# A last down product with tokens on the partitions

## What is computed

```python
def swiglu_2(h, w_in, w_out):
    gate, up = jnp.split(h @ w_in, 2, axis=-1)
    return (jax.nn.silu(gate) * up) @ w_out

x = x + 0.5 * swiglu_2(rmsnorm(x, ffn2_norm[l]), ffn2_w_in[l], ffn2_w_out[l])
return rmsnorm(x, final_norm)        # x * rsqrt(mean(x*x over 1024) + 1e-6) * final_norm
```

## Time and profile before

| | us |
|---|---|
| median of 3 runs (lowest, highest) | 1096.36 (1095.93, 1096.79) |
| the profiled execution's own time | 1097.15 |
| its span, first to last instruction | 1095.4 |
| PE busy, of the span | 1079.4 (99%) |
| DVE busy | 780.0 (71%) |
| ACT busy | 619.1 (57%) |
| POOL busy | 201.7 (18%) |
| mean granted TensorE clock, core 0 | 0.994 |

### The profile page before, as it was taken

The page is one execution under the profiler, slowest core; times in us unless marked ns, Lnnn a source line. Parts: engine busy times, 40 slices in busy tenths (PEclk is TensorE's granted clock), DMA queues, the critical chain, the costliest instruction groups (busy, mean ns, idle before and its releaser), DMA issues.

```text
span 1095.4 us, 17872 instructions
## 1 busy us (share of the span) xinstructions
PE 1079.4 (99%) x6282; PEld 945.1 (86%) x6282; DVE 780.0 (71%) x1097; ACT 619.1 (57%) x947; POOL 201.7 (18%) x213
## 2 busy tenths in 40 slices
PE   8999999998999999999999999999999999999997
PEld 6888888887888888888888888889988898888886
DVE  6866667687797666768666676788867669666664
ACT  7655544564676555447555545755655557555541
POOL 4311100026031111011111100133201012111100
PEclk9999999998999999999999999999999999999998
DMA  8755566552246555556555654655455546655561
GB/s 281 276 193 186 180 192 192 176 168 99 98 158 212 189 190 191 176 174 215 190 190 189 189 187 163 212 186 194 158 190 177 189 155 193 210 188 188 180 194 39
DMA packets 55571, 200.02 MB, mean 183 GB/s; under 512 B 6304, under 2 KB 6304, under 8 KB 55392
## 3 DMA queue, kind: packets, MB, share of 16 engines
q1 hardware_dynamic: 54576, 196.11, 54.8%
q0 software_dynamic: 512, 2.65, 0.6%
q10 hardware_dynamic: 432, 0.57, 0.2%
HBM read 198.26 MB, written 1.05 MB: 182 GB/s over the span
## 4 chain that ended last, share of the span: by engine, by line
PE 93%; DVE 3%; POOL 1%; ACT 1%; DMA 1%; issue 0%; ACTq 0%; DVEq 0%; POOLq 0%
PE pair L1247 53%; PE pair L1248 27%; PE pair L1241 4%; PE pair L1243 4%; PE pair L1242 4%; DVE x_hl L817 1%; DVE w_lo L811 1%; PE pair L1460 1%; DMA x<-x_in 1%; POOL x_sq L395 1%; POOL x_sq L387 1%; PE pair L1470 0%; DVE x L828 0%; PE pair L1523 0%; PE pair L1565 0%
## 5 line engine op out<-in xcount | busy, mean ns | idle before, releaser
L811 DVE TENSOR_TENSOR w_lo<-w_raw,w_hi 128x1024 fp32r<-128x1024 f32 x369 | 462.2, 1259 | 230.4 <-ACT w_hi L463 229.8
L1247 PE MATMUL pair<-x_hl,w_hi 128*128 128x512 f32 x1728 | 604.2, 395 | 2.6 <-DVE x_hl L817 1.6
L463 ACT ACTIVATE w_hi<-w_raw 128x1024 fp32r<-128x1024 f32 x369 | 385.9, 1056 | 241.9 <-PE pair L1248 201.6
L1248 PE MATMUL pair<-x_hl,w_lo 128*128 128x256 f32 x1728 | 482.1, 279 | 0.0
L1247 PEld LDWEIGHTS pair<-x_hl,w_hi 128*128 128x128 f32 x1728 | 323.8, 187 | 79.2 <-DVE w_lo L811 2.0
L1248 PEld LDWEIGHTS pair<-x_hl,w_lo 128*128 128x128 f32 x1728 | 325.7, 188 | 0.1
L1247 PE MATMUL pair<-wide,w_hi 128*128 128x512 f32 x832 | 289.8, 393 | 0.0
L1248 PE MATMUL pair<-wide,w_lo 128*128 128x256 f32 x832 | 232.0, 279 | 0.0
L1247 PEld LDWEIGHTS pair<-wide,w_hi 128*128 128x128 f32 x832 | 155.9, 187 | 35.7
L1248 PEld LDWEIGHTS pair<-wide,w_lo 128*128 128x128 f32 x832 | 156.8, 188 | 0.0
L347 POOL TENSOR_TENSOR wide<-hid_b,wide 128x256 fp32r<-128x256 f32 x88 | 86.5, 984 | 374.7 <-ACT wide L525 374.7
(11 more groups left out here) (183 smaller groups left out, 846.4 us busy)
## 6 DMA issues: line engine op xcount, KB each, us to landing
w_raw<-stream SPq DMA_DIRECT2D x369, 512.0 KB, 4.2
const<-const_in POOLq DMA_DIRECT2D x1, 1248.0 KB, 8.6
w_raw<-stream SPq DMA_DIRECT2D x4, 256.0 KB, 5.6
out<-x_sq SPq DMA_DIRECT2D x4, 256.0 KB, 2.6
rows<-rows_in POOLq DMA_DIRECT2D x1, 576.0 KB, 10.6
x<-x_in ACTq DMA_DIRECT2D x2, 256.0 KB, 5.7
x<-x_in SPq DMA_DIRECT2D x2, 256.0 KB, 6.9
sgu_w<-sgu_w_in POOLq DMA_DIRECT2D x1, 512.0 KB, 13.6
```

The lines of the kernel that those rows point to most:

```text
L463: nc.scalar.activation(w_hi[:, slot, :], w_raw[:, slot, :], ACT.Copy).then_inc(w_hi_done, 1)
L811: nc.vector.tensor_tensor(w_lo[:, slot, :], w_raw[:, slot, :], w_hi[:, slot, :].bitcast(F32), ALU.subtract).then_inc(w_split, 1)
L1247: nc.tensor.matmul(dst, a_hi, b_hl.rearrange("p a s -> p (a s)"), start=first, stop=False, skip_group_check=True)
L1248: return nc.tensor.matmul(dst[:, 0:S], a_lo, b_hl[:, 0, :], start=False, stop=last, skip_group_check=True)
```

## The change

The down product of the last layer (p = 5) turns round; those of the other three layers stay.

- **Start.** TensorE transposes `x` (16 transposes of 128 x 128, into banks 0 to 3) and `rstd` (2, into bank 5). ACT copies the transposed `x` to `y_tok`, four times 128 x 512. DVE makes `r_col` = 0.5 x the first column of each transposed `rstd`.
- **Product.** Activations of 128 tokens are stationary, 512 weight columns move. For each half h of the features: 22 hidden chunks x 2 token groups x `three`. The host lays out the last 22 blocks to suit. Half 0 goes to banks 4 and 6, half 1 to banks 0 and 2. In half 1 the last four hidden chunks are done for the first token group, then for the second.
- **Half 0** is finished in the middle of the product: DVE adds `bank * r_col` to `y_tok`, ACT squares with an accumulated sum, DVE multiplies by the gain.
- **The end.** Per token group DVE makes the residual of half 1, ACT squares it with its sum, DVE multiplies by the gain; a root and its inverse are made for a column of 128 x 1; ACT scales half 0 and stores it from its own queue, DVE scales half 1 and SP stores it.
- The gain row comes by one more DMA of 512 KB from POOL, after `add_squares(5)`. The output has token rows. The sum over partitions, the diagonal and its product are gone.

```diff
@@ sync @@
-            for c in range(4):
-                sp.wait_ge(out_ready, c + 1)
-                sp.dma_start(out[:, 2 * c:2 * c + 2, :], x_sq[:, 2 * c:2 * c + 2, :]).then_inc(stored, 16)
+            for t in range(TT):
+                sp.wait_ge(out_ready, t + 1)
+                sp.dma_start(out[:, t, 512:D], out_tok[:, t, :]).then_inc(stored, 16)
@@ gpsimd @@
             add_squares(5)
+            pool.wait_ge(ya_split, KC)
+            pool.dma_start(gain_row, gain_in).then_inc(gain_loaded, 16)
             hidden_lo(3)
@@ scalar, ffn @@
+                def token_square(t, h):
+                    act.wait_ge(y_tok_made, TT * h + t + 1)
+                    nc.scalar.activation(q_tok[:, t, :], y_tok[:, t, 512 * h:512 * h + 512], ACT.Square,
+                                         accum_out=(end_part, end_sum)[h][:, t:t + 1]).then_inc(end_sq, 1)
+                def store(t):
+                    act.wait_ge(end_r_done, t + 1)
+                    act.wait_ge(end_gained, t + 1)
+                    nc.scalar.activation(y_tok[:, t, 0:512], y_tok[:, t, 0:512], ACT.Identity,
+                                         scale=end_r[:, t:t + 1]).then_inc(out_act_ready, 1)
+                    act.wait_ge(out_act_ready, t + 1)
+                    act.dma_start(out[:, t, 0:512], y_tok[:, t, 0:512]).then_inc(stored, 16)
                 if p == 5:
+                    for t in range(TT):
+                        act.wait_ge(x_T, t + 1)
+                        for h in range(2):
+                            nc.scalar.activation(y_tok[:, t, 512 * h:512 * h + 512], bank[2 * t + h][:, :],
+                                                 ACT.Copy).then_inc(x_T_copied, 1)
+                    for b in range(1, FC):
+                        split(n0 + UP_B + b + 3)
+                        if b == FC // 2:
+                            for t in range(TT):
+                                token_square(t, 0)
+                    for t in range(TT):
+                        token_square(t, 1)
+                        end_root_of(t)
+                        store(t)
+                    return
@@ vector, ffn @@
+                def token_residual(t, h):
+                    if h == 0:
+                        dve.wait_ge(w_used, n0 + UP_B + FC // 2)
+                    elif t == 0:
+                        dve.wait_ge(first_tokens, 1)
+                    else:
+                        dve.wait_ge(w_used, n0 + FFN_B)
+                    half = y_tok[:, t, 512 * h:512 * h + 512]
+                    nc.vector.scalar_tensor_tensor(half, bank[4 - 4 * h + 2 * t][:, :], r_col[:, t:t + 1], half, ALU.mult,
+                                                   ALU.add).then_inc(y_tok_made, 1)
+                    token_residual(0, 1)
+                    second_half_gain(0)
+                    end_scale(0)
+                    token_residual(1, 1)
+                    second_half_gain(1)
+                    store(0)
+                    end_scale(1)
+                    store(1)
@@ tensor @@
+            def tokens_down(n0):
+
+                pe.wait_ge(parts_added, 4 * FC - 2)
+                for t in range(TT):
+                    for c in range(KC):
+                        last = nc.tensor.transpose(bank[2 * t + c // 4][:, c % 4 * P:(c % 4 + 1) * P],
+                                                   x[:, c, t * P:(t + 1) * P], ident)
+                    last.then_inc(x_T, 1)
+                pe.wait_ge(parts_added, 4 * FC - 1)
+                for t in range(TT):
+                    last = nc.tensor.transpose(bank[5][:, t * P:(t + 1) * P], rstd[:, t * P:(t + 1) * P], ident)
+                last.then_inc(rT_done, 1)
+
+                def chunk(k, h, t):
+                    n, w = n0 + UP_B + (FC * h + k) // 2, slice(k % 2 * 512, k % 2 * 512 + 512)
+                    pe.wait_ge(w_split, n + 1)
+                    if h == 0 and t == 0:
+                        pe.wait_ge(hid_split, 3 * FC + k + 1)
+                    tok = slice(t * P, (t + 1) * P)
+                    return three(bank[4 - 4 * h + 2 * t][:, :], hid_hi[:, k, tok], hid_lo[:, k, tok], w_hi[:, n % RING, w],
+                                 w_lo[:, n % RING, w], k == 0, k == FC - 1)
+
+                for k in range(FC):
+                    for t in range(TT):
+                        if k == 0 and t == 1:
+                            pe.wait_ge(parts_added, 4 * FC)
+                        last = chunk(k, 0, t)
+                    if k % 2:
+                        last.then_inc(w_used, 1)
+                pe.wait_ge(x_T_copied, 2 * TT)
+                for k in range(FC - 4):
+                    for t in range(TT):
+                        last = chunk(k, 1, t)
+                    if k % 2:
+                        last.then_inc(w_used, 1)
+                for t in range(TT):
+                    for k in range(FC - 4, FC):
+                        last = chunk(k, 1, t)
+                        if t and k % 2:
+                            last.then_inc(w_used, 1)
+                    if t == 0:
+                        last.then_inc(first_tokens, 1)
...
-            for k in range(KC):
-                pe.wait_ge(x_sq_done, KC * 6 + k + 1)
-                for t in range(TT):
-                    last = nc.tensor.matmul(bank[4][:, t:t + 1], x_sq[:, k, t * P:(t + 1) * P], ones[:, 0:1],
-                                            start=(k == 0 and t == 0), stop=(k == KC - 1), skip_group_check=True)
-            last.then_inc(sumsq_done, 1)
```

More of the change, by code:

```diff
@@ L74, with build @@
 UNSEL, NEG, MASKED = -3.0e38, -2.0e38, -1.0e30
-def build(nc, stream, x_in, cols_in, rows_in, const_in, sgu_w_in, pool_w_in, out):
+def build(nc, stream, x_in, cols_in, rows_in, const_in, sgu_w_in, pool_w_in, gain_in, out):
     ctx = ExitStack()
@@ new lines, in end_scale @@
+                def end_scale(t):
+                    one = slice(t, t + 1)
+                    dve.wait_ge(end_sq, TT + t + 1)
+                    nc.vector.scalar_tensor_tensor(end_ms[:, one], end_sum[:, one], 1.0 / D, end_part[:, one], ALU.mult,
+                                                   ALU.add).then_inc(end_ms_done, 1)
+                    dve.wait_ge(end_root_done, t + 1)
+                    inv_root(end_ms[:, one], end_root[:, one], end_nt[:, one], end_r[:, one]).then_inc(end_r_done, 1)
@@ new lines, in store @@
+                def store(t):
+                    dve.wait_ge(end_r_done, t + 1)
+                    nc.vector.tensor_scalar(out_tok[:, t, :], out_tok[:, t, :], end_r[:, t:t + 1], None,
+                                            ALU.mult).then_inc(out_ready, 1)
+                if p == 5:
+                    dve.wait_ge(rT_done, 3)
+                    for t in range(TT):
+                        nc.vector.tensor_scalar(r_col[:, t:t + 1], bank[5][:, t * P:t * P + 1], 0.5, None,
+                                                ALU.mult).then_inc(half_r_made, 1)
+                    for b in range(1, FC):
+                        split(n0 + UP_B + b + 3)
+                        if b == FC // 2:
+                            dve.wait_ge(half_r_made, TT)
+                            dve.wait_ge(x_T_copied, 2 * TT)
+                            dve.wait_ge(gain_loaded, 16)
+                            for t in range(TT):
+                                token_residual(t, 0)
+                        if b == FC // 2 + 1:
+                            for t in range(TT):
+                                first_half_gain(t)
+                    dve.wait_ge(end_part_done, TT)
+                    token_residual(0, 1)
[6 more added lines that the diff above has]
+                    store(1)
+                    return
@@ L1219, in _ @@
             ffn(3, START[5], 5)
[L1221 to L1224, removed]
-            for t in range(TT):
[L1226 to L1233, removed]
-                                        ALU.mult).then_inc(out_ready, 1)
         @block.tensor
@@ L1353, in ffn @@
                         chunk(LEAD + j, j, i)
+                if p == 5:
+                    tokens_down(n0)
+                    return
                 for m in range(KC):
@@ L1560, in _ @@
             ffn(3, START[5], 5)
-            for k in range(KC):
-                pe.wait_ge(x_sq_done, KC * 6 + k + 1)
-                for t in range(TT):
-                    last = nc.tensor.matmul(bank[4][:, t:t + 1], x_sq[:, k, t * P:(t + 1) * P], ones[:, 0:1],
-                                            start=(k == 0 and t == 0), stop=(k == KC - 1), skip_group_check=True)
-            last.then_inc(sumsq_done, 1)
-            for t in range(TT):
-                pe.wait_ge(diagonal_done, t + 1)
-                last = nc.tensor.matmul(bank[5][:, t * P:(t + 1) * P], ones[:], newton[:, t * P:(t + 1) * P],
-                                        start=True, stop=True, skip_group_check=True)
-            last.then_inc(spread_done, 1)
 MIX1_SPLITS = (1, 2, 4, 7, 9)
@@ L1689 @@
     y = r.results[0]["out"]
```

(1 more changed line is left out.)

76 lines of the change are left out of this document (47 added, 29 removed).

## The result

The changed kernel took 1102.11 us (median of 22 runs, 1095.34 to 1105.59), the kernel before beside it 1096.14 (22 runs, 1095.66 to 1100.27). The ratio is 1.0041, 95% interval 1.003 to 1.0052. (A ratio with an interval is here an estimate from all runs of both kernels, not the quotient of the medians, which is 1.0054.) So the change costs 6 us between the medians and some 4.5 by the ratio, where a gain of 3.7, to 1092.7, was forecast. New as well is the scatter: 10 us between runs of the same program.

The account below looks back on a forecast made before the run. TensorE's stream was taken to bound the kernel up to the last down product's end, then a 12.1 us tail. Tail -4.56, product -1.08 and transposes +1.98 made -3.66, from 1096.36 to 1092.7 us; range 1091.5 to 1095.2.

Parts of the forecast that it names:

- Start: Start of the last down product: eighteen new transposes on TensorE at 0.11 us each add 1.98 us, with no wait.
- Product: Last down product: 264 matmuls at 0.227 us take 59.94 us against 61.02, a gain of 1.08.
- Cover: Beside the product: weight splits resume at about 1030.1, margin 2.8 us; mid-product they run 2.6 late of 6.0 allowed.
- Rival (a): Start or middle of the product: the weight ring runs dry behind ACT's waits, costing up to 2.4 us (1095.1); chance 0.06.
- Tail: After the last matmul: 7.34 us from when DVE may read it to the span's end; tail balance -4.56.
- Rival (b): Transposes at the product's start: TensorE's clock falls to half rate, losing 3.45 us (1096.15); chance 0.08.
- Rival (c): Early last layer: the gain's DMA delays the weight stream, TensorE stands for 4.8 us (1097.5); chance 0.04.
- Rival (d): Last down product: the turned form is no faster, giving 1093.8; counted within the forecast's 0.82.
- The first step of the prediction: Up to the last down product's end, 1083.30, only TensorE's stream counts: 176 pairs of 0.3467 us from 1022.28.
- the start of the sum: Start of the last down product at 1022.28 us, taken unchanged from the kernel before.

Follow-up runs that it names:

- e4: The kernel before, with the gain row's 512 KB DMA added, loaded and not used; median 1096.05 us against 1096.15, ratio 0.9988.
- e12: e2 with `ones` 64 bytes higher, again on a multiple of 64, and `wide` 128 bytes further from the weights; median 1095.9 us, ratio 0.9985 to before.
- e2: The changed kernel with every tile padded back to its old place; median 1093.0 us, ratio 0.9959 to before.
- e14: e12 with `wide` moved another 128 bytes on; median 1092.8 us, ratio 0.996 to before.
- e17: e2 with everything from `w_hi` on (split weights, `x_hl`, `wide`) 128 bytes higher, distances kept; median 1092.6 us, ratio 0.9965 to before.
- e9: The same kernel as e2, run again on another chip; median 1095.9 us, ratio 0.9984 to before.
- e1: The changed kernel unaltered, run again; median 1097.4 us (1093.1 to 1104.8), ratio 1.0001 to before.
- e11: e2 with only `ones` 32 bytes off, and `wide` 128 bytes further from the weights; median 1099.7 us, ratio 1.0023 to before.
- e10: The same kernel as e6, run again on another chip; median 1099.6 us, ratio 1.0017 to before.
- e15: e11 with `wide` moved another 128 bytes on; median 1096.3 us, ratio 0.9985 to before.
- e16: e2 with `x_hl` and all behind it 128 bytes on, and `wide` another 128 on; median 1102.1 us, ratio 1.0045 to before.
- e6: The changed kernel with only `ones` put back to its old place (padding also pushed `wide` by 128 bytes); median 1098.8 us, ratio 0.999 to before.
- e7: The kernel before with the six other moved tiles 32 bytes off, `ones` kept aligned, `wide` pushed 256 bytes; median 1096.7 us, ratio 0.997.
- e3: The kernel before with all seven moved tiles 32 bytes off (padding also pushed `wide` by 128 bytes); median 1105.3 us, ratio 1.0072.
- e5: The kernel before with only `ones` 32 bytes off (padding also pushed `wide` by 128 bytes); median 1104.7 us, ratio 1.0044.
- e8: e2 with one more, unused matmul of `ones` ahead of the second mixer's pairs; median 1096.5 us, ratio 0.9965 to before.
- e18: e12 with `wide` moved another 192 bytes on; median 1096.0 us, ratio 0.9994 to before.
- e13: The kernel before with 128 bytes of padding ahead of `wide`, moving it and the tiles behind it; median 1104.2 us, ratio 1.0048.

## Why the prediction was wrong

**What held.** In the profiled execution, step by step:

- *Start:* 18 transposes in 1.98 us; they took 1.88 (1031.69 to 1033.57), no wait with them.
- *Product:* 59.94; it took 59.96.
- *Cover:* the splits of weights were to begin again 7.8 us after the product's start, and did after 7.2; in the middle they came 1.6 late, of 6.0 allowed. Rival (a) did not happen.
- *Tail:* 7.34 from the moment the last matmul can be read; 1100.9 - 1093.73 = 7.17. The residual took 0.75 (0.74), the last issue on ACT's queue came at 1097.70, +3.97 as worked out, and ACT's second square stood behind its first store. ACT's scaling cost more (0.72 for 0.63), the stores less.
- *Rival (b):* granted clock 1.00 over the transposes. The Trainium skill's rule (TensorE: Matmul & The Clock Gate, "Part 4: PE-mode transpose"), by which they do not count as activity in the way that matmuls do, had no effect on the grant in these 1.9 us. *Rival (c):* e4, no effect. (Its waits would have stood some 110 us before the product, not before the end as I wrote: the DMA was issued at 918.41.) *Rival (d):* 0.227, not 0.231, at this distance of the tiles; with another distance (e12) it would have been right.

From the product's start to the end this makes -3.9 where -3.66 was forecast. And with well placed tiles the whole kernel comes to the forecast of 1092.7: 1093.0 (e2), 1092.8 (e14), 1092.6 (e17), though once 1095.9 (e9).

**What failed.** The first step of the prediction: "So up to the product's end only TensorE's own stream counts", and with it the start of the sum, 1022.28, which I carried over as a constant. That TensorE bounds these stages was right; that its stream takes the same time when its instructions are the same was not: +9.4 us. No term or rival allowed for it, and my range of 3.7 us was about one slow layer wide. Two things could have warned me. Before runs in its second mixer the same pairs at 353.3 ns that its layers run at 346.7; I read one rate and took it for the rate. And the diff takes 8 columns from `cols`, which I did not name as a part.

**How sure the cause is.** Shown: in the profiled pair the loss is the slow rhythm in three unchanged layers; the gain's DMA does not bring it (e4); in the changed kernel, tiles 32 bytes off cost 3.5 to 4.4 us on three chips (e1 against e2, e11 and e10 against e12, e15 against e14, the last with intervals that just overlap). The rates point the same way: with `ones` 32 off, gate and up ran slow in 14 of 24 profiled layers, otherwise in 10 of 52 (e16 left out), 4 of these in e6 and e10. Shown too is that it is a matter of odds, as the same program ran at 1093 and at 1104. Open: how much of the 6 us of the first comparison was placement and how much the draw of that chip, since e1 had a ratio of only 1.0001; which tiles count besides `ones` (e10 lost with the six others out of line, e7 lost nothing with the same in before); and what in the chip makes the rhythms. A clean test of the 32 bytes in the kernel before is lacking, since `wide` moved with it in e3 and e5.

**Versions that beat before:** the changed kernel with constants at multiples of 64 bytes and the old distances, modulo 256, of `x_hl` and `wide` from the weights: e2, e14 and e17, at 0.996 of before, with upper ends of 0.9974 to 0.9984 (e9, the same kernel as e2, reaches 1.0003). Of these only e2 had the changed kernel itself (e1) beside it. Such ratios hang on how before fares on the chip: on that of e5 to e8 its median was 1099.56, and even e7, before with other places, came to 0.997 of it.

## What to carry to other kernels

Before a change of a few us is credited or blamed, compare the untouched stages of the two traces at common milestones. If they differ, see whether the change moved tiles: the size of one small tile shifts all that are allocated behind it, and padding to the old places is a test of a few lines. Then look at what the padding itself moves; mine changed the rates of six kernels by accident.

## What the runs showed of the hardware

- A steady stream of these matmuls on TensorE has several stable rhythms at full granted clock. Pairs of 512 and 256 columns: 346.7, 351.1 or 353.3 ns (e18 showed some 349 too). Matmuls of 512 columns, each with its own weight load: 226.7, 232.3 or 233.3 ns. Where they were written out, their patterns repeat to a nanosecond or two, and one matmul of another kind can switch them (e8).
- The distance between the moving tile and the weights, modulo 256 bytes, decided in every execution whether the 351.1 and 232 to 233 ns appeared (e13, e16, e17): always at +128, never at 0 or +256 (at +320: 349 and 233.3). The Trainium skill (SBUF — State Buffer, "Operand start alignment") treats start addresses as a question of what is legal and says that its runs timed nothing; here 128 bytes between two tiles cost 3.1 us of 1096 in the down products alone (e13).
- In the mixers the first matmul with `ones` started 233 to 235 ns after the matmul before it in all six executions with `ones` 32 off a multiple of 64, and 226 to 229 ns after it in 13 of the 14 others (e16: 233), from the records.
- Eighteen transposes in a row, 109 ns apart, left the granted clock at 1.00.
